# Two-layer hybrid encoder in split fp32: pool tile copied out of PSUM by ScalarE, decay scans moved to the end of a pair, state products moved behind the gate tile

## The reference

```python
q, k, v, ga, u, gp, z, xbc, dt_raw, gl = split(h @ w_in[l])
ya = sliding_window_attention(q, k, v) * silu(ga)          # A
yb = multiscale_pool(u, pool_w, pool_scale) * silu(gp)     # B
yc = ssd_branch(z, xbc, dt_raw)                            # C
g  = sigmoid(gl)                                           # 3 x 1024
merged = g0 * (ya @ w_pa) + g1 * (yb @ w_pb) + g2 * (yc @ w_pc)
x = x + gate * (merged @ w_out)
```

## Time and profile before

| | |
|---|---|
| median of 3 runs | 1277.31 us (1276.59 to 1281.36) |
| profiled execution | 1277.12 us, its span 1275.2 us |
| TensorE (PE) busy | 1164.0 us, 91% |
| VectorE (DVE) busy | 591.3 us, 46% |
| ScalarE (ACT) busy | 509.2 us, 40% |
| GpSimd (POOL) busy | 522.4 us, 41% |
| mean granted TensorE clock | 0.963 of full |
| DMA | 139.18 MB, 109 GB/s mean |

### The profile page before, as it was taken

How to read it: one execution, slowest core, us unless ns; L and a number is a source line. 1 busy time by engine, 2 the same in 40 slices (tenths; PEclk the granted TensorE clock), 3 DMA queues, 4 the chain that set the end, 5 groups by cost and what they waited for, 6 DMA issues and landing times. The chain is left out here.

```text
span 1275.2 us, 14923 instructions
## 1 busy us (share of the span) xinstructions
PE 1164.0 (91%) x5906; PEld 957.4 (75%) x5906; DVE 591.3 (46%) x741; ACT 509.2 (40%) x872; POOL 522.4 (41%) x392
## 2 busy tenths in 40 slices
PE   3289999997998899999989999999799989999996
PEld 2278888886877787788767888888677868778875
DVE  6744225655657552322435223655567554232334
ACT  2135326763433443322334434655344343232322
POOL 1534434442332344544542443534233234555540
PEclk9579999998999999999999999999899999999998
DMA  9824642332444223333224452223424413333321
GB/s 358 277 59 121 197 132 67 83 84 83 108 124 112 54 75 99 108 99 99 83 71 104 134 193 82 83 83 99 110 57 120 120 50 99 91 100 100 99 83 66
DMA packets 211461, 139.18 MB, mean 109 GB/s; under 512 B 11417, under 2 KB 203969, under 8 KB 209345
## 3 DMA queue, kind: packets, MB, share of 16 engines
q1 hardware_dynamic: 209968, 133.52, 36.4%
q10 hardware_dynamic: 1424, 4.72, 1.0%
HBM read 135.08 MB, written 2.62 MB: 108 GB/s over the span
## 5 line engine op out<-in xcount | busy, mean ns | idle before, releaser
L428 POOL TENSOR_TENSOR w_lo<-raw,w_hi 128x512 fp32r<-128x512 f32 x360 | 496.7, 1402 | 694.9 <-ACT w_hi L726 694.9
L461 PE MATMUL main<-h_hi,w_hi 128*128 128x512 f32 x1184 | 475.7, 402 | 38.4 <-DVE misc L1170 27.9
L461 PE MATMUL main<-h_hi,w_lo 128*128 128x512 f32 x1184 | 465.3, 393 | 0.0
L461 PE MATMUL main<-h_lo,w_hi 128*128 128x512 f32 x1184 | 465.3, 393 | 0.0
L726 ACT ACTIVATE w_hi<-raw 128x512 fp32r<-128x512 f32 x360 | 207.6, 623 | 391.1 <-PE main L461 331.9
L461 PEld LDWEIGHTS main<-h_hi,w_hi 128*128 128x128 f32 x1184 | 225.4, 190 | 97.7 <-DVE misc L1170 30.7
L461 PEld LDWEIGHTS main<-h_hi,w_lo 128*128 128x128 f32 x1184 | 225.0, 190 | 48.5
L461 PEld LDWEIGHTS main<-h_lo,w_hi 128*128 128x128 f32 x1184 | 225.6, 191 | 47.2 <-issue 1.9
L1223 DVE TENSOR_TENSOR tmp<-main,misc 128x512 f32<-128x512 f32 x32 | 22.1, 691 | 202.0 <-PE main L461 202.0
L461 PE MATMUL main<-y_hi,w_hi 128*128 128x512 f32 x256 | 101.6, 397 | 1.4 <-DVE y_lo L1229 1.4
L1072 DVE SCALAR_TENSOR_TENSOR misc<-main,lcol,misc 128x511 f32<-128x511 f32 (+2 forms) x96 | 71.9, 749 | 65.1 <-ACT misc L726 62.5
(11 more groups left out here) (185 smaller groups left out, 997.1 us busy)
## 6 DMA issues: line engine op xcount, KB each, us to landing
raw<-in_w_in SPq DMA_DIRECT2D x132, 512.0 KB, 3.9
zs<-in_w_ada SPq DMA_DIRECT2D x8, 1024.0 KB, 7.8
big<-in_w_ada SPq DMA_DIRECT2D x8, 1024.0 KB, 9.0
xbc<-in_w_ada SPq DMA_DIRECT2D x16, 512.0 KB, 4.7
raw<-in_w_pc SPq DMA_DIRECT2D x16, 512.0 KB, 3.7
raw<-in_w_out SPq DMA_DIRECT2D x16, 512.0 KB, 3.7
tmp<-step_rows SPq DMA_DIRECT2D x8, 512.0 KB, 4.1
big<-step_rows SPq DMA_DIRECT2D x8, 512.0 KB, 5.3
```

Of the source, the lines that this page charges most:

```text
L428: nc.gpsimd.tensor_tensor(w_lo[:, b, k:k + BT_, :], raw[:, b, k:k + BT_, :], w_hi[:, b, k:k + BT_, :].bitcast(F32), ALU.subtract).then_inc ...
L461: return nc.tensor.matmul(o, a, b_, start=start, stop=stop)
```

## The change

ScalarE gets a copy of `main[0]` into `u_sb[p]` right after tile (u,0), and this copy counts `s_evac[0]`. The rounding of weights (u+1,0) moves from behind the exps to behind that copy, ahead of the exps. VectorE's pooling reads `u_sb[p]` instead of `main[0]`, and its last instruction counts a new semaphore, `s_pool`, for which `pool_mm` waits. The two decay scans of pair p+1 go behind L1201 of pair p, ahead of `merge_a(1)`; those of pair 0 go ahead of the loop. On TensorE `states` stands behind tile (u+1,0) in pairs 1 and 2 as it did in pair 0. On VectorE L1186 goes ahead of the state update. `u_sb` are three slots of the 10x512 buffer and half of `buf_r`, none of them new memory.

```diff
+        u_sb = [qkv[:, 0], qkv[:, 2], qkv[:, 4], buf_r[:, 512:1024]]
...
             def pool_mm(l, p):
-                pe.wait_ge(s_evac[0], l * COUPLES + U_MIX + p * MIX + 1)
+                pe.wait_ge(s_pool, l * PAIRS + p + 1)
...
                     if p > 0:
                         y_off(l, p)
-                        if p < PAIRS - 1:
-                            states(l, p)
                     h_tile(l, u + 1, 0)
-                    if p == 0:
+                    if p < PAIRS - 1:
                         states(l, p)
                     y_diag(l, p)
...
                     w_hi_part(l, u, 1)
+                    act.wait_ge(s_tile[0], l * COUPLES + u + 1)
+                    f(u_sb[p], main[0][:, :], ACT.Copy).then_inc(s_evac[0], 1)
+                    w_hi_part(l, u + 1, 0)
                     for half in range(2):
                         act.wait_ge(s_diff, (l * PAIRS + p) * 2 + half + 1)
                         f(decay[half], decay[half], ACT.Exp).then_inc(s_dec, 1)
...
-                    w_hi_part(l, u + 1, 0)
                     evac(u, 1, pgate, ACT.Silu, BT_)
...
+                def seg_sums(p):
+                    for half in range(2):
+                        dve.wait_ge(s_srow[half], (l * PAIRS + p + 1) * 16)
+                        nc.vector.tensor_tensor_scan(out=decay[half], data0=decay[half], data1=seg0[:, :],
+                                                     initial=NEG_INF, op0=ALU.add, op1=ALU.max).then_inc(s_diff, 1)
...
-                    dve.wait_ge(s_tile[0], l * COUPLES + u + 1)
-                    ch.link(nc.vector.tensor_tensor_scan(out=csum[:, 16:16 + SEQ], data0=main[0][:, :],
+                    dve.wait_ge(s_evac[0], l * COUPLES + u + 1)
+                    ch.link(nc.vector.tensor_tensor_scan(out=csum[:, 16:16 + SEQ], data0=u_sb[p],
...
-                    tt(pooled[:, 0:16], few, main[0][:, 0:16], ALU.subtract).then_inc(s_evac[0], 1)
-
+                    tt(pooled[:, 0:16], few, u_sb[p][:, 0:16], ALU.subtract).then_inc(s_pool, 1)
+
+                    if p > 0:
+                        dve.wait_ge(s_yo, l * (PAIRS - 1) + p)
+                        dve.wait_ge(s_erow, (l * (PAIRS - 1) + p) * 32)
+                        ch.link(tt(buf_w, buf_w, psB[:, :], ALU.mult))
                     if p < PAIRS - 1:
                         dve.wait_ge(s_st, l * (PAIRS - 1) + p + 1)
...
+                    dve.wait_ge(s_yd, l * PAIRS + p + 1)
                     if p == 0:
-                        dve.wait_ge(s_yd, l * PAIRS + p + 1)
                         y_sum = psA
                     else:
-                        dve.wait_ge(s_yo, l * (PAIRS - 1) + p)
-                        dve.wait_ge(s_erow, (l * (PAIRS - 1) + p) * 32)
-                        ch.link(tt(buf_w, buf_w, psB[:, :], ALU.mult))
-                        dve.wait_ge(s_yd, l * PAIRS + p + 1)
                         ch.link(tt(buf_w, buf_w, psA[:, :], ALU.add))
...
                     tt(at(y_lo, p + BT_), buf_b, at(y_hi, p + BT_).bitcast(F32), ALU.subtract).then_inc(s_yb, 1)
+                    if p < PAIRS - 1:
+                        seg_sums(p + 1)
                     merge_a(1)
...
-                for p in range(PAIRS - 1):
+                seg_sums(0)
+                for p in range(PAIRS):
                     mix(p)
-                mix(PAIRS - 1)
```

More of the change, by code:

```diff
@@ L229, in build @@
         s_yn, s_y = sem("y_norm_product"), sem("y_normed")
-        s_pm = sem("pool_product")
+        s_pm, s_pool = sem("pool_product"), sem("pooled_done")
         s_yb32, s_ybh, s_yb = sem("yb_f32"), sem("yb_hi_done"), sem("yb_ready")
@@ L1125, in merge_a @@
                     def merge_a(m):
+                        dve.wait_ge(s_pool, l * PAIRS + p + 1)
                         dve.wait_ge(s_tile[1], l * COUPLES + u + (2 + m))
@@ L1129, in merge_a @@
                         tt(at(merged, p * 2 + m), main[1][:, :], gate, ALU.mult).then_inc(s_evac[1], 1)
[L1131 to L1135, removed]
                     dve.wait_ge(s_xtr, l * PAIRS + p + 1)
@@ L1168, in mix @@
                     ch.link(stt(pooled, pooled, at(icnt, p)[:, 15:16],
-                                main[0][:, :], ALU.mult, ALU.subtract))
-                    tt(pooled[:, 0:16], few, main[0][:, 0:16], ALU.subtract).then_inc(s_evac[0], 1)
+                                u_sb[p], ALU.mult, ALU.subtract))
+                    tt(pooled[:, 0:16], few, u_sb[p][:, 0:16], ALU.subtract).then_inc(s_pool, 1)
[3 more added lines that the diff above has]
+                        ch.link(tt(buf_w, buf_w, psB[:, :], ALU.mult))
                     if p < PAIRS - 1:
```

## The result

| | before | after |
|---|---|---|
| median | 1276.95 us (4 runs, 1276.39 to 1281.36) | **1238.42 us** (4 runs, 1237.72 to 1240.66) |
| ratio | | 0.970 (95% interval 0.968 to 0.972) |
| profiled execution, its span | 1277.12 us, 1275.2 us | 1237.72 us, 1235.8 us |
| mean granted TensorE clock | 0.963 | 0.970 |

The changed kernel is 38.5 us faster; between the two profiled executions it is 39.4 us. Forecast were 34.2 us. (The kernel before has one run more here than in the table ahead of the prediction, 1276.39 us.)

The account below looks back on a forecast made before the run. TensorE's mix-stage waits (35.6 us) and slow clock after them (6.3) put 41.9 us at stake; less 1.7 + 1.1, 0.1 and 4.8 this leaves 34.2, so 1277.1 becomes 1242.9 us, range 1236 to 1251.

Parts of the forecast that it names:

- rival A: Pair ends and layer 1's pair 0: scans don't hold POOL, 3.8 and 0.5 us less, 1238.6 us; chance 0.22.
- What bounds it, and the 41.9 us: Mix stage: TensorE waits for pooling, state products and x*dt, 35.6 us, plus 6.3 us of slow clock after long stalls.
- The copy: After tile (u,0): eight ScalarE copies out of PSUM, 0.58 us each, covered by a 5.6 us tile, free main[0].
- Weights of pair 0: Pair 0's gate tile still waits for its late-landing, split weights: 1.7 us in layer 0, 1.1 in layer 1.
- rival B: Short stalls bring back the low clock or grow: gain shrinks 6 to 10 us, 1248.9 to 1252.9; chance 0.21.
- Exps and W: Pair 0: exps behind the weight conversion make W three us later, at 309.0; cost before states 0.1 us.
- State update 0.5 us late: Pairs 1 and 2: state update waits for states, so the sum with psA, y_sum and next weights come 0.5 us late.
- The scan holds POOL: Ends of pairs 1 and 2: POOL's subtraction waits out the second scan, stalling TensorE 1.25 us; 4.8 us over four ends.
- The scans no longer stand ahead of x*dt: Pairs 1 to 3: with 4.5 us of scans moved, waits before states (6.3 us) and y_off (1.4 us) go.
- C: Waits move rather than vanish: gate weights late in all pairs lose half the gain, 17 us, 1260 us; chance 0.04.
- D: Slower: pair ends wait for decay rows landing 14 us later than now, 1284 us; chance 0.02.

Follow-up runs that it names:

- no_copy: The changed kernel without ScalarE's copy: pooling reads main[0] again and its last instruction frees the bank; 1269.25 us, ratio 0.994.
- weights_first: The changed kernel with pair 0's gate weights issued ahead of both decay-row loads on the SP queue; 1235.35 us, ratio 0.967.
- scans_at_start: The changed kernel with the two decay scans back at the start of each pair, ahead of x*dt; 1257.84 us, ratio 0.984.
- copy_only: The kernel before with only the copy, the weight rounding behind it and VectorE's order of L1186; 1260.74 us, ratio 0.987.

## Why the prediction was right

The time lies in the range, but outside the band that I gave the forecast itself (1240.5 to 1245.5), and beside rival A (1238.6). That it meets A is luck: POOL does stand behind a scan, and other terms made up for it. By TensorE's starts in both traces the mix stages won 39.7 us, 5.5 more than forecast: the waits removed in pairs 1 to 3 gave 3.4 more, the ends of pairs 1 and 2 cost 2.4 less, pair 0 up to y_diag gave 0.9 more, and the ends of pair 0 cost 1.2 that I had at nothing. By the steps:

- **What bounds it, and the 41.9 us.** Right in what waits for what, too small in the sum. The view counts an idle from the modelled end of a matmul, 0.39 us after its start, while the next one in a stream starts after 0.23: that is 0.16 us a wait. Behind y_off's small products it is 0.25: for the states of pair 1 the view has 1.51 us, but from y_off's start to the next work's it is 3.46 us before and 1.70 after, so 1.76 were won (first the rows before, then after):

```profile
347.11 1.95 PE L461 MATMUL psB<-xbc,tmp 128*128 128x128 f32 x16
350.57 1.97 PE L461 MATMUL psC<-tmp 128*128 128x256 f32 x8 [1.51 <-issue]
```
```profile
340.69 1.95 PE L462 MATMUL psB<-xbc,tmp 128*128 128x128 f32 x16
342.39 0.48 PE L462 MATMUL main<-h_hi,w_hi 128*128 128x512 f32 x1
```

  Over pairs 1 to 3 of both layers, up to y_diag, 26.7 us were won where the terms have 23.3, in 13 waits: 0.26 us each. Part of it is that a tile behind a wait takes 5.67 us where it takes 5.56 without one (342.39 to 347.95, changed kernel).
- **The copy.** Right in mechanism: no_copy loses 31 us. Its cost of nothing held: no wait of TensorE for the copy appears.
- **Weights of pair 0.** 1.7 and 1.1 us forecast, 1.44 and 0.67 measured, and weights_first shows that the queue ahead of the load is the cause. In layer 1 POOL did stand behind the second scan as assumed, for some 0.3 us (its two subtractions take 2.87 us, 2.52 in layer 0). The slow clock did not follow (rival B falls): 5.63 us for the gate tile, granted clock 1.00.
- **Exps and W.** W ended at 308.13 + 1.21 = 309.3 and states started at 309.44. The stage began 0.66 us later in this execution, so both are 0.3 us earlier than reckoned, as the weights were, and states start 0.1 us behind W as forecast.
- **State update 0.5 us late.** Right where it arises, mis-sized behind it. L1190 (L1188 before) started 2.61 us after y_diag's first matmul (352.38 against 349.77), not 2.08 (361.45 against 359.37). But L1203 was only 0.14 us late, because L1198 lost less of its time to a POOL subtraction that had begun earlier, 1.72 us against 2.09:

```profile
352.38 1.21 DVE L1190 TENSOR_TENSOR tmp<-tmp,psA 128x1024 f32<-128x1024 f32 x1
...
356.34 1.72 DVE L1198 TENSOR_TENSOR xbc<-xbc,zs 128x1024 f32<-128x1024 f32 x1
...
359.70 0.69 DVE L1203 TENSOR_TENSOR y_lo<-tmp,y_hi 128x512 fp32r<-128x512 f32 x1 [0.98 <-ACT y_hi L725]
...
362.51 2.27 DVE L1124 TENSOR_TENSOR_SCAN big<-big,seg 128x1024 f32<-128x1024 f32 x1
365.65 0.69 DVE L1136 TENSOR_TENSOR big<-main,misc 128x512 f32<-128x512 f32 x1 [0.87 <-PE main L462]
```
```profile
363.81 3.30 POOL L429 TENSOR_TENSOR w_lo<-raw,w_hi 128x512 fp32r<-128x512 f32 x2 [6.83 <-ACT w_hi L725]
```

- **The scan holds POOL.** The mechanism was right and **the size was wrong: 1.25 us a pair end forecast, 0.6 measured** (y_diag's first matmul to the next tile's, 16.23 us after, 359.37 to 374.99 = 15.62 before). The rows above, changed kernel, end of pair 1, show why. POOL begins at 363.81, inside the scan that ends at 364.78; the two subtractions take 3.30 us where they took 2.55, so it did stand, 0.75 us. But the scan ended 0.4 us earlier than reckoned, since VectorE was not 0.5 us late, and the first half was through 1.06 us after it (363.81 + 3.30 - 1.27 = 365.84), not 1.27. Four ends at 0.6 instead of 1.2 are 2.4 of the 5.5 us. At the ends of pair 0, forecast even, it is the same from the norm product to the next `to_tokens`: 9.98 us before, 10.57 after, in both layers. With waits of 0.30 us there by the view, two such ends take 1.2 us back. Scans held between 3.3 and 3.4 us in two experiments bear out what the Trainium skill (SBUF — State Buffer, Who interferes with whom) says of VectorE with two SBUF inputs: a scan is such an instruction.
- **"The scans no longer stand ahead of x*dt"** was given as the reason why 7.7 us of waits go. It was too weak. With the copy in place the scans' old position costs 19.4 us, and in pairs 1 to 3 some four fifths of its cost is the lock (16.7 of 20.5 us): the edit that brings the rounding forward sends POOL into them. I priced what the moved rounding does in the kernel as changed, never what it would have done to the scans in their old place, and so missed why the change is made of these two parts.
- **Rivals C and D**: no trace of either. VectorE's idle before merge_a(1) was 0.87 us (forecast 0.5), and no wait for step_rows stands at a pair's end.
- **Not tested.** The rounding's move was not undone in the kernel as changed, with the scans at the pair's end, nor was the new place of L1186. What these two are worth by themselves stays open.

## What to carry to other kernels

A bank that a slow reader holds is worth a cheap copy by an idle engine, but then follow the work that was waiting behind it: here the freed weight conversion ran into another engine's scans and, had the scans stayed where they were, half the gain (19.4 of 38.5 us) would have been lost again, most of it by the lock. Before moving an instruction on GpSimd or its feeder, list the VectorE instructions with two SBUF inputs that it will now stand beside. And of a change in several parts, undo each alone: one of the three undone here did nothing where the other two stood.

## What the runs showed that I had not expected

- Tiny instructions pay the full price of the lock. The 128x16 product (L1169), 0.17 us by itself in pairs 1 to 3, took 1.13 us in pair 0 of both layers of the changed kernel, next to a POOL subtraction:

```profile
310.63 1.58 DVE L1167 TENSOR_TENSOR misc<-big 128x512 f32<-128x512 f32 x1
312.25 1.13 DVE L1169 TENSOR_TENSOR sm<-misc,icnt 128x16 f32<-128x16 f32 x1
```
```profile
310.28 3.07 POOL L429 TENSOR_TENSOR w_lo<-raw,w_hi 128x512 fp32r<-128x512 f32 x2 [1.68 <-ACT w_hi L725]
```

- The length of a stall does not settle the clock behind it. A wait of 2.40 us before y_off in scans_at_start was followed by products at full speed (2.05 us for sixteen, granted clock 1.00), one of 2.39 us in copy_only by slow ones (granted 0.50 from 343.2 to 345.3):

```profile
342.49 2.05 PE L462 MATMUL psB<-xbc,tmp 128*128 128x128 f32 x16 [2.40 <-DVE tmp L1140]
```
```profile
342.19 3.15 PE L462 MATMUL psB<-xbc,tmp 128*128 128x128 f32 x16 [2.39 <-DVE tmp L1142]
```
